# Turning the softmax rows of the memory attention: VectorE's 32x32 turns and a trip through DRAM in place of TensorE's transposes

## What is computed

```
def memory_attention(q, k, v):            # q: (1, 4, 1024, 64); k, v: (1, 4, 256, 64)
    logits = einsum('bhqd,bhkd->bhqk', q, k) * 64 ** -0.5
    p = softmax(logits, axis=-1)          # every token reads all 256 memory tokens
    return einsum('bhqk,bhkd->bhqd', p, v)
...
y = concat(stick_breaking heads (8), forgetting heads (8), memory heads (4))
y = rmsnorm_per_head(y) * silu(gate);  x = x + y @ w_out;  return rmsnorm(x)
```

## Time and profile before

| | |
|---|---|
| time, median of 3 runs | 783.72 us (783.58 to 783.74) |
| profiled execution: time, span | 784.63 us, 781.8 us |
| granted TensorE clock | 1.000 (2.4 GHz) |
| busy: PE, DVE, ACT, POOL | 770.8, 609.5, 445.7, 262.6 us |
| DMA | 101.64 MB, mean 130 GB/s |

### The profile page before, as it was taken

How to read it: one execution, slowest core, us unless ns; L and a number is a source line. 1 busy time by engine, 2 the same in 40 slices (tenths; PEclk the granted TensorE clock), 3 DMA queues, 4 the chain that set the end, 5 groups by cost and what they waited for, 6 DMA issues and landing times.

```text
span 781.8 us, 11859 instructions
## 1 busy us (share of the span) xinstructions
PE 770.8 (99%) x3966; PEld 646.5 (83%) x3966; DVE 609.5 (78%) x1206; ACT 445.7 (57%) x920; POOL 262.6 (34%) x440
## 2 busy tenths in 40 slices
PE   8999999999999999999999999999999999999997
PEld 8878888888888888888888888888888888888885
DVE  6886687766789977778997877899777679885776
ACT  7767764556656555675646566565555474642233
POOL 0112724252247326223832431384225133310000
PEclk9999999999999999999999999999999999999999
DMA  9413864234125424522361443235233498235323
GB/s 346 148 49 139 274 207 123 68 82 135 68 68 143 141 55 109 135 68 68 100 176 50 122 96 107 68 95 130 93 89 85 109 370 304 95 133 178 131 101 141
DMA packets 79948, 101.64 MB, mean 130 GB/s; under 512 B 39048, under 2 KB 55432, under 8 KB 78864
## 3 DMA queue, kind: packets, MB, share of 16 engines
q1 hardware_dynamic: 79888, 100.89, 41.8%
HBM read 66.11 MB, written 25.85 MB: 118 GB/s over the span
## 4 chain that ended last, share of the span: by engine, by line
PE 86%; DVE 6%; DMA 2%; ACT 2%; issue 2%; POOL 1%; SPq 0%; DVEq 0%; ACTq 0%; POOLq 0%
PE banks L904 15%; PE banks L906 15%; PE banks L905 15%; PE banks L949 11%; PE banks L1070 8%; PE banks L1090 4%; PE banks L1056 4%; PE banks L1057 4%; PE banks L1089 4%; PE banks L1110 2%; PE banks L1141 1%; DMA hT<-wo_dram 1%; DVE sb_heads L1764 1%; DVE pT L1905 1%; DMA yT<-in_mem 1%
## 5 line engine op out<-in xcount | busy, mean ns | idle before, releaser
L904 PE MATMUL banks<-hT,w_parts 128*128 128x512 f32 x576 | 237.5, 412 | 0.3 <-DVE sb_heads L1764 0.2
L906 PE MATMUL banks<-hT,w_parts 128*128 128x512 f32 x576 | 225.8, 392 | 0.0
L905 PE MATMUL banks<-hT,w_parts 128*128 128x512 f32 x576 | 225.3, 391 | 0.0
L1295 ACT ACTIVATE pT<-banks 128x512 fp32r<-128x512 f32 x208 | 92.5, 498 | 120.1 <-PE banks L1070 119.8
L1905 DVE TENSOR_TENSOR pT<-banks,pT 128x512 fp32r<-128x512 f32 x208 | 108.2, 562 | 56.9 <-ACT pT L1295 55.7
L906 PEld LDWEIGHTS banks<-hT,w_parts 128*128 128x128 f32 x576 | 108.1, 188 | 24.5
L904 PEld LDWEIGHTS banks<-hT,w_parts 128*128 128x128 f32 x576 | 108.5, 188 | 16.5 <-DVE sb_heads L1764 1.0
L905 PEld LDWEIGHTS banks<-hT,w_parts 128*128 128x128 f32 x576 | 108.9, 189 | 13.5
L1563 POOL TENSOR_TENSOR w_parts<-w_raw,w_parts 128x1024 fp32r<-128x1024 f32 x34 | 82.0, 2412 | 90.4 <-ACT w_parts L1198 90.4
L1570 POOL TENSOR_SCALAR_AFFINE_SELECT work<-work 128x128 f32<-128x128 f32 x64 | 35.8, 559 | 182.2 <-ACT work L1272 182.2
L1865 DVE TENSOR_TENSOR_SCAN work<-work 128x639 f32<-128x639 f32 (+3 forms) x64 | 90.7, 1417 | 3.6 <-POOL work L1570 3.5
(11 more groups left out here) (254 smaller groups left out, 1345.2 us busy)
## 6 DMA issues: line engine op xcount, KB each, us to landing
w_raw<-in_w_tiles SPq DMA_DIRECT2D x36, 512.0 KB, 3.7
hT<-wo_dram SPq DMA_DIRECT2D x14, 512.0 KB, 7.8
fx_heads<-fx_heads SPq DMA_DIRECT2D x8, 512.0 KB, 6.7
negL<-negL_dram SPq DMA_DIRECT2D x8, 512.0 KB, 5.4
yT_dram<-silu SPq DMA_DIRECT2D x8, 512.0 KB, 4.0
sb_heads<-sb_heads SPq DMA_DIRECT2D x8, 512.0 KB, 7.2
negL<-yT_dram SPq DMA_DIRECT2D x8, 512.0 KB, 4.5
work<-in_x SPq DMA_DIRECT2D x6, 512.0 KB, 7.4
```

The costliest lines, as they stand in the source:

```text
L904: pe.matmul(o, w[0][:, k, :], hT[:, 0, k, tok], start=(k == 0), stop=False)
L905: pe.matmul(o, w[0][:, k, :], hT[:, 1, k, tok], start=False, stop=False)
L906: mm = pe.matmul(o, w[1][:, k, :], hT[:, 0, k, tok], start=False, stop=(k == KT - 1))
L1295: act.activation(pT[:, n % 3, 0, cols], banks[:, T_BANK + n % 2, cols], ACT.Copy).then_inc(t_hi, 1)
```

## The change

For the memory groups TensorE transposes nothing any more. As soon as a unit's exponentials are there, DVE turns each 32x32 block of its rows (`turn_probabilities`, 128x8x32) and writes the blocks of the four units interleaved into `work`. When a group's four units are turned, ACT issues four DMAs that store them to a new DRAM tensor `p_dram` (`store_turned`, tick 4g+5, after the exponentials of that tick), each from 32 partitions, in rows of 512 bytes and of 128 KB in all; the DRAM rows then stand in the order of memory tokens. In tick 4g+6, after the exponentials, ACT waits until all four have landed and issues two DMAs that fetch the two steps into `pT` (`fetch_turned`, 256 KB each). In tick 4g+7 `upper_part` waits for each step to land and rounds it from `pT` to `pT`; DVE subtracts; PE's value products of the group stand at the end of tick 4g+8, where they stood at the end of 4g+6. The output is written at tick 4g+9 as before, with its columns put in order. The exponentials go to two alternating rows outside the turned area and wait for an earlier turn (`p_turned`); the counts of `t_ready` start after the memory steps; `plan` spreads the same parts a little differently over the ticks of the memory phases, with no total or end changed.

```
-        row = (0 if group % 2 == 0 else 3328) + j * MEM
+        row = j * MEM if group == 0 else (3072, 4352)[j % 2]
...
     if x.kind == "mm":
-        return 4 * t.group + 5
+        return 4 * t.group + 7
...
+        def p_turned_of(g):
+            return work[:, 3328 * (g % 2):3328 * (g % 2) + 4 * MEM]
...
             def transposes(n):
+                if UNIT[u].kind == "mm":
+                    return
...
             def exponentials(u):      # ScalarE
-                    if rows_free(u):
-                        act.wait_ge(t_ready, rows_free(u))
+                    if u >= 6:
+                        act.wait_ge(p_turned, u - 1)
                     act.activation(p_row(u), banks[:, S_BANK + CHUNK0[u] % 2, 0:MEM], ACT.Exp, bias=top,
                                    accum_out=total).then_inc(fx_p, 1)
...
+            def store_turned(g):
+                act.wait_ge(p_turned, 4 * g + 4)
+                rows = p_dram[g, :, :].rearrange("(k a) (i n) -> i a k n", a=Q4, i=P // Q4)
+                for i in range(P // Q4):
+                    act.dma_start(rows[i], p_turned_of(g)[i * Q4:(i + 1) * Q4, :].rearrange("a (k n) -> a k n", k=MEM // Q4)).then_inc(p_out, 16)
+
+            def fetch_turned(g):
+                act.wait_ge(p_out, 64 * (g + 1))
+                for n in range(STEP0[g], STEP0[g + 1]):
+                    if n >= 3:
+                        act.wait_ge(pv_done, n - 2)
+                    act.dma_start(pT[:, n % 3, 1, :].bitcast(F32), p_dram[g, STEP[n].s * P:(STEP[n].s + 1) * P, :]).then_inc(p_in[STEP[n].s], 16)
+
             def upper_part(n):
+                if n < N_MEM_STEPS:
+                    act.wait_ge(p_in[STEP[n].s], 16 * (STEP[n].group + 1))
+                    act.activation(pT[:, n % 3, 0, :], pT[:, n % 3, 1, :].bitcast(F32), ACT.Copy).then_inc(t_hi, 1)
+                    return
...
+                if i % 4 == 1 and 0 <= i // 4 - 1 < N_MEM_GROUPS:
+                    store_turned(i // 4 - 1)
+                if i % 4 == 2 and 0 <= i // 4 - 1 < N_MEM_GROUPS:
+                    fetch_turned(i // 4 - 1)
...
+            def turn_probabilities(u):      # VectorE
+                t = UNIT[u]
+                dve.wait_ge(fx_p, fx_no(u) + 1)
+                if t.group >= 2:
+                    dve.wait_ge(p_out, 64 * (t.group - 1))
+                place = p_turned_of(t.group).rearrange("p (k j b) -> p j k b", j=4, b=Q4)[:, t.j, :, :]
+                dve.transpose(place, p_row(u).rearrange("p (k b) -> p k b", b=Q4)).then_inc(p_turned, 1)
...
             def lower_part(n):
+                if n < N_MEM_STEPS:
+                    dve.tensor_tensor(pT[:, n % 3, 1, :], pT[:, n % 3, 1, :].bitcast(F32), pT[:, n % 3, 0, :].bitcast(F32),
+                                      ALU.subtract).then_inc(t_lo, 1)
+                    return
...
+                if 1 <= i <= 4 * N_MEM_GROUPS:
+                    turn_probabilities(i - 1)      # last in VectorE's tick i
```

More of the change, by code:

```diff
@@ L104, in t_tick @@
     if x.kind == "mm":
-        return 4 * t.group + 5
+        return 4 * t.group + 7
     return 4 * t.group + 5 + (t.s // 2 if x.c else t.s // 2 * 2)
+N_MEM_GROUPS = sum(1 for g in range(N_GROUPS) if UNIT[4 * g].kind == "mm")
+N_MEM_STEPS = STEP0[N_MEM_GROUPS]
 T_AT = [[k for k in range(len(STEP)) if t_tick(k) == i] for i in range(N_TICKS)]
@@ L368, in hybrid_layer @@
     part_dram = nc.dram_tensor("part_dram", (4, P, D), F32, kind="Internal").ap()
+    p_dram = nc.dram_tensor("p_dram", (N_MEM_GROUPS, MEM, CW), F32, kind="Internal").ap()
     v_dram = nc.dram_tensor("v_dram", (N_PH, 2, CW, P), F32, kind="Internal").ap()
@@ L552, in hybrid_layer @@
         diag_ready, fx_max, fx_p = sem("diag_ready"), sem("fx_max"), sem("fx_p")
+        p_turned, p_out, p_in = sem("p_turned"), sem("p_out"), [sem(f"p_in{b}") for b in range(MB)]
         t_ready, t_hi, t_lo, pv_done = sem("t_ready"), sem("t_hi"), sem("t_lo"), sem("pv_done")
@@ L588, in rows_free @@
             t = UNIT[u]
-            if t.group < 2:
-                return 0
-            if "mm" in (t.kind, UNIT[4 * (t.group - 2)].kind):
-                return STEP0[t.group - 1]
-            return STEP0[t.group - 2] + 4 * t.c + t.j + 1
+            return STEP0[t.group - 2] - N_MEM_STEPS + 4 * t.c + t.j + 1
         def bank_of(q):
@@ L775, in load_part @@
                 sp.wait_ge(part_out[X_STAGE[n]], 16 * x_turn(n))
-                sp.wait_ge(t_ready, len(STEP) if n == 3 else STEP0[N_GROUPS - 1])
+                sp.wait_ge(t_ready, (len(STEP) if n == 3 else STEP0[N_GROUPS - 1]) - N_MEM_STEPS)
                 sp.dma_start(res[n], part_dram[n, :, :]).then_inc(pb_in[n], 16)
@@ L1263, in sigmoids @@
                     act.wait_ge(small_done, small_of("N3", 0, t.ph - 2) + 1)
[L1264 to L1265 removed]
+                act.wait_ge(t_ready, rows_free(u))
                 f, b = f_row(n), p_row(u)
@@ L1874, in logits @@
                 t = UNIT[u]
-                dve.wait_ge(t_ready, rows_free(u))
+                if t.group < N_MEM_GROUPS + 2:
+                    dve.wait_ge(p_out, 64 * (t.group - 1))
+                else:
+                    dve.wait_ge(t_ready, rows_free(u))
                 dve.wait_ge(diag_ready, causal_no(u) + 1)
@@ L1913, in output @@
                     dve.wait_ge(gy_done, 2 * (t.ph - 1) + TURN[t.c] + 1)
-                dve.tensor_tensor(yT[mine, t.c * CW:(t.c + 1) * CW], banks[mine, O_BANK, :], o_tmp[other, :],
-                                  ALU.add).then_inc(o_read, 1)
+                y, o, add = yT[mine, t.c * CW:(t.c + 1) * CW], banks[mine, O_BANK, :], o_tmp[other, :]
+                if t.kind == "mm":
+                    y = y.rearrange("p (j i b) -> p i j b", j=4, b=Q4)
+                    o, add = [v.rearrange("p (i j b) -> p i j b", j=4, b=Q4) for v in (o, add)]
+                dve.tensor_tensor(y, o, add, ALU.add).then_inc(o_read, 1)
             def y_lo(n):
```

10 lines of the change are left out of this document (5 added, 5 removed).

## The result

| | before | after |
|---|---|---|
| time, median | 783.67 us (783.58 to 783.74, 4 runs) | 835.25 us (833.96 to 837.03, 4 runs) |
| ratio, 95% interval | | 1.0656 (1.0642 to 1.0671) |
| profiled execution: time, span | 784.63, 781.8 us | 833.96, 832.2 us |
| mean granted clock | 1.000 | 0.971 |

A forecast was written before the change was run, and what follows sets the result against it. PE's instruction stream was taken to bound the kernel. Store-to-store cycles of 4 x 13 + 2 x 10.1 us put PE 18.7 late at tick 32; less 0.8 for group 7's transposes, +17.9 gave 801.6 us, range 787 to 817.

The forecast's parts named there:

- the first store: Group 0's first store on ACT was to go out 1.6 us after unit 4's scores, at 69.4.
- those of groups 4 and 5: Store-to-store cycles in the quiet stretch, taken at the quiet price of 10.1 us each.
- The price of groups 0 to 3: Store-to-store cycles in the loaded stretch: 13 us each taken, between 10.1 quiet and 16.6 loaded.
- the loaded price of these legs: Under DMA load, the four stores, issue and landing, were to take 6.3 us, the fetch 7.4.
- The last leg: Second rounding 0.60, second lower part 0.69, DVE's turn, maximum and turn 1.45, handoffs 0.2: 2.94 us before the next store.
- ACT's own exponentials behind the rounding fit beside that: In the cycle's last leg, ACT's exponentials were to fit beside DVE's turn, maximum and turn.
- PE isn't in this cycle.: PE's scores for the next units are long done; PE meets the store-to-store cycle only at the value products.
- The 6.3 us of the transposes: Removing 64 transposes, 8 blocks of 0.79 us, was to take 6.3 us off PE.
- I leave their durations: Rounding and lower part, now reading `pT` instead of PSUM, were to stay at 0.60 and 0.69 us.
- The slow clock: Rival: PE's pauses drop the granted clock to 1.2 GHz in the memory phases, 19 us more, 821; chance 0.08.
- The loaded price in full: Rival: groups 0 to 3 take four cycles of 16.6 us, 14.4 more, 816.0; within the forecast's 0.81.
- All hidden: Rival: shortest transfer times give a 7.7 us cycle, PE keeps pace, 6.3 us gained, 777.4; faster side's chance 0.09.

The follow-up runs named there:

- experiment 7: The changed kernel with the first five w_out tiles stored with 32 of their 1024 columns, 5 MB less traffic: 825.91 us, 1.0539.
- experiment 12: Same number of transfers, but small: in the changed kernel 823.97 us; with fetch to output two ticks later 806.31; in the kernel before, with nobody reading them, 791.07.
- Experiment 6: The changed kernel with the same stores, fetches and waits at the same ticks, but in SyncE's program in place of ScalarE's: 826.08 us, 1.0542.
- experiment 2: The changed kernel without stores, fetches and VectorE's 32 turns, exponentials going straight to the place that is rounded: 784.43 us, 1.0008.
- experiment 3: The kernel before, with the memory groups' lower part subtracting from probability rows in SBUF instead of the transposes' PSUM bank: 786.68 us, 1.0040.
- experiment 8: The changed kernel plus sixteen unread filler matmuls of 512 columns ahead of the scores of ticks 7, 12, 16 and 20: 835.40 us, 1.0658.
- experiment 10: The changed kernel with fetch, rounding, value products and output of groups 0 to 6 two ticks later: 811.53 us, 1.0358.
- experiment 14: The changed kernel, fetch to output two ticks later, next group's stores moved behind the rounding: 813.77 us, 1.0375; with small transfers 804.94 us, 1.0267.

## Why the prediction was right in sign and wrong in size

**The ledger of the medians.** These are differences of medians from different chips, on which the kernel before took 783.65 to 784.04. Transposes left out, later value products, lower parts from SBUF: +0.7 (784.43). Turns: +3.2 (787.59). Trip: +47.7 (835.25); 15.2 of it is there when nobody waits, and 23.7 go away with two ticks of room.

**The ledger in the prediction's terms.** Tick 33 starts 51.4 us late, where 18.7 was forecast for the end of tick 32. The other 32.7 us are: the first store, 4.4 (73.75 for 69.4); the cycles of groups 0 to 3, 20.6 (72.6 for 52); those of groups 4 and 5, 3.2 (12.0 and 11.3 for 10.1 each); from the store of group 6 to tick 33, 4.6 (14.4 for 9.4 and the 0.4 that lay between the ticks before), whose cause I haven't followed.

**Right.** PE's stream set the end, and what makes PE wait there is lost for good: tick 33 is 51.4 us late, the median 51.6. ACT waits in its own program for two transfers one after the other, and this lengthens the cycle from store to store beyond PE's 7.6 us. In all eight groups the first store goes out within 0.04 us of the end of the fourth unit's turn, as forecast. A turn takes 0.44 us on DVE, also as forecast. The rounding takes 0.62, for 0.60.

**The price of groups 0 to 3 (forecast 13 us a cycle).** This is the step that failed first. I had both ends, 10.1 and 16.6, and chose 13 since the rate of the stretch is reached only in parts. The four cycles took 72.6 us together, 18.2 each. From the first store to the rounding they took 13.1, 13.8, 10.7 and 15.4, on average 13.2, which is the loaded price of these legs (6.3 + 7.4 = 13.7). Moving off it cost 4 x 3.6 = 14.4 us of forecast. That the sum fits so well is in part luck. From the first store to the first fetch's issue it took 10.5, 6.9, 7.4 and 8.7, on average 8.4 for 6.3, and from there to the rounding 2.6, 6.9, 3.3 and 6.6, on average 4.9 for 7.4: two errors cancel. And the load wasn't what I took it for: with 5 MB of it gone the cycles were still 16 us on average (experiment 7), and with small transfers 15.7 (experiment 12). I had scaled a landing by its size and its neighbours, and most of the price goes with neither the trip's bytes nor this part of the load. Whether it goes by the number of transfers, by the two waits in a row or by the load that was left, no run separates.

**The last leg (forecast 2.94 us).** From the first rounding to the next store it took 5.7, 3.6, 5.7 and 4.6, and in the quiet stretch 5.4, 4.5 and 7.2. This is the second step that failed. The order on DVE was right (lower part, turn, maximum, turn, store), but I had put only these four in the leg, though I had counted 7.7 us of work for DVE and 8.7 for ACT in 7.6. In the cycle shown above ACT's `w_out` split (1.04) and two copies of a projection (0.58 and 0.59) stand behind the rounding, two additions on DVE wait for the copies, and the fourth turn stands behind those. There the sentence "ACT's own exponentials behind the rounding fit beside that" failed:

```profile
90.70 0.68 DVE L1802 TENSOR_TENSOR fx_heads<-banks,fx_heads 64x512 fp32r<-64x512 f32 x1 [0.94 <-ACT fx_heads L1226]
...
92.13 0.45 DVE L1942 STREAM_TRANSPOSE work<-work 128x256 f32<-128x256 f32 x1
```

In groups 2 to 6 it held, and ACT even waited for DVE's maximum, 0.6 to 5.1 us a group, for example:

```profile
126.11 0.47 ACT L1293 ACTIVATE work<-banks,npeak 128x256 f32<-128x256 f32 x1 [3.75 <-DVE npeak L1933]
```

Here DVE was late. In group 2 its two lower parts took 3.81 us beside GpSimd for some 1.3 (the lines are at the end), in group 6 3.15; in group 3 a turn and a sum of phase 0's norm (0.70 and 0.69) stand ahead of the fourth turn; in groups 4 and 5 the lower part started 1.6 and 1.3 us after its rounding was done, behind other work of DVE. In group 1, the shortest, the second rounding came 1.0 us after the first.

The first store is a reading that failed: I took the 1.09 us from scores to exponentials from unit 19, and unit 4's exponentials already start at 71.28 in the kernel before, 3.5 us after their scores, behind a scan on DVE (2.27 us) and ACT's copies.

**"PE isn't in this cycle."** Right for the cycle: the maxima on DVE waited 0.9 us in all for PE's scores from 66 to 190 us. Wrong in what follows it, that PE's scores for the next units are long done and that it meets the cycle at the value products only. Exponentials stand behind the stores' issue and behind the fetch's wait, and scores of unit u need those of unit u-2. So PE waited 26.9 us at scores and 10.0 at value products. Experiment 6 bears it out from the other side: with ACT free the scores hardly wait any more, though the sum stays.

**The 6.3 us of the transposes.** Not obtained. "I leave their durations" failed for the lower part: 1.00 us on average for 0.69, since it now has two inputs in SBUF and stands still beside GpSimd (+2.8 us of time alone), and the products two ticks later cost 1.7 alone. I had looked for what the new instructions cost, and not for what an old one costs from another source. The two add to 4.5 us and not to the 7 of experiment 2, where five pairs of lower parts took 2.25 to 3.49 us and not one as in experiment 3; the 6.3 itself was read from eight transposes of one tick and never measured by itself. This is left open.

**The rivals.** *The slow clock* had the right condition, a clock down to 0.68 in a window, and not the mechanism: filler matmuls raised it and gave nothing back (experiment 8). That its 821 lies nearest to 835 is luck. *The loaded price in full* (816.0) had the right mechanism and was 19 us short. *All hidden* was far off: even with nothing transferred the kernel is slower than before by 0.5%.

**The rule on issuing engines.** The Trainium skill ("DMA: Bandwidth & Descriptors", section "Issuing engines are not separate DMA queues") says that DMAs from several engines run on the same 16 DMA engines, so that a second issuing engine saves only the time to issue. Experiment 6 agrees with it: all transfers in one queue were no slower than in two, but 9 us faster. It also says that the time to issue is usually small beside the transfer. In group 1 that holds for one DMA (1.87 us for four, 0.47 each). In group 0 the trace differs: four took 5.53 us, 1.4 each, and that is half the median landing over all groups, 2.8 us:

```profile
p_dram<-work ACTq DMA_DIRECT2D x32, 128.0 KB, 2.8
pT<-p_dram ACTq DMA_DIRECT2D x16, 256.0 KB, 2.9
```

**Open.** With room and small transfers 18.7 us above the kernel without the trip remain (806.31 against 787.59). Some 7 are the small transfers as such (experiment 12); that the rest is one queue's order, I tried and could not show (experiment 14). Fewer transfers per group, GpSimd's queue, or the trip with no other traffic beside it were not tried.

## What to carry to other kernels

Before a step is moved into an engine's queue, list everything that stands behind each of its waits and each of its issues, and follow who needs that: here the stores' issue and two waits for DMAs on ACT became 26.9 us of waits of TensorE at a place that the forecast held for safe. A leg of a cycle is not the sum of the instructions that one follows; whatever else stands between them in the queue belongs to it. When a term of a sum has a loaded and a quiet price and the trace shows the stretch to be loaded, take the loaded one, and expect that even it is short; cutting the bytes of this round trip to an eighth and a quarter took off only 11.3 of its 47.7 us. And a saving counts only once the instructions that stay have been looked at from their new sources and at their new time.

## What the runs showed of the chip that I had not expected

- Issuing four stores of 128 KB took ACT 1.9 to 2.6 us in seven groups and 5.53 in the first (6.15 in experiment 10), beside SP's stores and loads of `w_out`. With five tiles of `w_out` stored light the first took 1.99. An eighth of the bytes took 1.74 at the least and 3.86 in the first. SP had the same, 1.86 to 6.11. A busy stretch alone doesn't make the issue long: group 1's, at 92.61, took 1.87.
- A lower part of 128x512 takes 0.65 to 0.69 us alone; beside a GpSimd operation on SBUF two of them took up to 3.84 us when both inputs were in SBUF, and 1.29 with one in PSUM. In the changed kernel:

```profile
121.42 3.81 DVE L1948 TENSOR_TENSOR pT<-pT 128x512 fp32r<-128x512 f32 x2 [4.92 <-ACT pT L1317]
...
121.87 2.81 POOL L1593 TENSOR_TENSOR w_parts<-w_raw,w_parts 128x1024 fp32r<-128x1024 f32 x1
```

- From 69 to 146 us, where PE paused for up to 5.9 us, the granted clock averaged 0.68 to 0.81, between the levels of 1.2 and 2.4 GHz (0.50 and 1.00), and matmuls of 512 columns took 0.63 us (at 80.54, right behind the wait of 5.44) where they take 0.39. PE was busy for 76.5 us from 69 us to tick 33, where it had been 63.0 with 64 transposes more. Still, raising the clock gave no time back (experiment 8).
